# Two layers of a hybrid decoder step: decode chain reordered, page turns over three banks, heads paired

## The reference

```python
def trunk_layer(h, p, pos0, past, weights):
    a = rmsnorm(h, g_attn)
    qa, ka, va, qi, ki, wi, qb, kb, vb, u = split_columns(a @ w_in)
    qa, ka, qi, ki = ...            # QK-norm of qa, ka; rotary of all four
    # A: indexer scores, top-k keys, softmax over the chosen keys
    score = einsum('bqhs,bqh->bqs', relu(einsum('bqhd,bsd->bqhs', qi, ki) * 64 ** -0.5), wi)
    sel = top_k(where(causal, score, -inf), min(256, L // 4))
    o_a = softmax(qa . k_sel / 8) @ v_sel                   # 6 query heads, 2 KV heads
    # B: stick-breaking attention, 6 heads
    z = einsum('bqhd,bshd->bhqs', qb, kb_f) / 8
    log_rem = where(strict, log_sigmoid(-z), 0)
    o_b = exp(where(strict, z + reverse_cumsum(log_rem), -inf)) @ vb_f
    # C: causal pooling mixer
    o_c = pool_mix(u_ext, pos, w_pool, pool_scale)
    h = h + concat(o_a, o_b, o_c) @ w_out
    y, new_conv = conv_ffn(rmsnorm(h), conv_prefix, w_up, conv_w, conv_b, w_down)
    h = h + y
    return h + sigmoid(rmsnorm(h) @ w_ple_gate) * (p @ w_ple_proj), ...
```

## Time and profile before

| | us |
|---|---|
| median of 3 runs | 1666.86 (1665.31 to 1668.43) |
| the profiled execution | 1670.36 |
| its span | 1668.6 |
| TensorE busy | 1594.0 (96%) |
| VectorE, ScalarE, GpSimd busy | 885.2, 684.4, 274.9 |
| mean granted clock of TensorE | 0.969 |

### The profile page before, as it was taken

The page is one execution under the profiler, slowest core; times in us unless marked ns, Lnnn a source line. Parts: engine busy times, 40 slices in busy tenths (PEclk is TensorE's granted clock), DMA queues, the critical chain, the costliest instruction groups (busy, mean ns, idle before and its releaser), DMA issues.

```text
span 1668.6 us, 30587 instructions
## 1 busy us (share of the span) xinstructions
PE 1594.0 (96%) x11750; PEld 1439.5 (86%) x11750; DVE 885.2 (53%) x1558; ACT 684.4 (41%) x989; POOL 274.9 (16%) x472
## 2 busy tenths in 40 slices
PE   7999978899999999999999999879999999999998
PEld 5787845699999999999978786458999999999998
DVE  6657885135555553322847588632455555522335
ACT  4444546244444442224443344543444444422241
POOL 3320250011111110000105105201111111100000
PEclk8999979799999999999999999879999999999999
DMA  5233043132233323323223311341233323233221
GB/s 174 57 91 83 26 138 90 36 89 79 85 88 88 88 85 97 91 83 89 77 80 93 103 39 54 91 106 52 76 89 88 88 87 89 77 101 92 86 77 59
DMA packets 225719, 140.24 MB, mean 84 GB/s; under 512 B 13122, under 2 KB 219604, under 8 KB 225552
## 3 DMA queue, kind: packets, MB, share of 16 engines
q1 hardware_dynamic: 223220, 133.46, 27.9%
q0 software_dynamic: 2400, 5.42, 1.1%
HBM read 131.21 MB, written 7.65 MB: 83 GB/s over the span
## 4 chain that ended last, share of the span: by engine, by line
PE 80%; DVE 11%; issue 3%; ACT 3%; SPq 1%; DMA 1%; POOL 0%; DVEq 0%; ACTq 0%; POOLq 0%
PE ps L1679 23%; PE ps L1681 23%; PE ps L1680 23%; DVE score L1342 2%; DVE m L1339 2%; DVE w_L L1241 1%; PE ps L1742 1%; PE ps L1828 1%; DVE Lb L1413 1%; PE ps L2073 1%; PE ps L1928 1%; DVE stat L1460 1%; PE ps L1706 1%; PE ps L1838 1%; PE ps L1840 1%
## 5 line engine op out<-in xcount | busy, mean ns | idle before, releaser
L1679 PE MATMUL ps<-bH,w_H 128*128 128x272 f32 x1664 | 481.0, 289 | 4.6 <-DVE w_L L1241 3.2
L1241 DVE TENSOR_TENSOR w_L<-w_raw,w_H 128x1024 fp32r<-128x1024 f32 (+4 forms) x236 | 257.3, 1099 | 422.9 <-ACT w_H L871 422.2
L1681 PE MATMUL ps<-bH,w_L 128*128 128x272 f32 x1664 | 479.6, 288 | 0.0
L1680 PE MATMUL ps<-bL,w_H 128*128 128x272 f32 x1664 | 477.8, 287 | 0.0
L871 ACT ACTIVATE w_H<-w_raw 128x1024 fp32r<-128x1024 f32 (+4 forms) x236 | 220.1, 943 | 286.8 <-PE ps L1681 286.5
L1679 PEld LDWEIGHTS ps<-bH,w_H 128*128 128x128 f32 x1664 | 312.5, 188 | 6.3 <-DVE w_L L1241 4.1
L1680 PEld LDWEIGHTS ps<-bL,w_H 128*128 128x128 f32 x1664 | 313.6, 188 | 0.1
L1681 PEld LDWEIGHTS ps<-bH,w_L 128*128 128x128 f32 x1664 | 312.6, 188 | 0.0
L1679 PE MATMUL ps<-actH,w_H 128*128 128x272 f32 x704 | 204.2, 290 | 0.0
L1681 PE MATMUL ps<-actH,w_L 128*128 128x272 f32 x704 | 203.8, 289 | 0.0
L1680 PE MATMUL ps<-actL,w_H 128*128 128x272 f32 x704 | 202.7, 288 | 0.0
(11 more groups left out here) (329 smaller groups left out, 2344.0 us busy)
## 6 DMA issues: line engine op xcount, KB each, us to landing
w_raw<-in_w_up SPq DMA_DIRECT2D x88, 512.0 KB, 3.8
w_raw<-in_w_down SPq DMA_DIRECT2D x32, 512.0 KB, 3.9
w_raw<-in_w_in SPq DMA_DIRECT2D x24, 512.0 KB, 4.5
w_raw<-in_w_ple_gate SPq DMA_DIRECT2D x16, 512.0 KB, 3.9
w_raw<-in_w_down SPq DMA_DIRECT2D x16, 384.0 KB, 3.4
w_raw<-in_w_out SPq DMA_DIRECT2D x16, 320.0 KB, 3.4
w_raw<-in_w_in SPq DMA_DIRECT2D x8, 452.0 KB, 3.9
w_raw<-in_w_in SPq DMA_DIRECT2D x8, 384.0 KB, 3.2
```

The source lines that it names most:

```text
L1241: ins = dve.tensor_tensor(w_L[u % SPLIT][:, a:b], w_raw[raw_slot(l, u)][:, a:b], w_H[u % SPLIT][:, a:b].bitcast(F32), ALU.subtract)
L1679: pe.matmul(out, wh, xh, start=start, stop=False)
L1680: pe.matmul(out, wh, xl, start=False, stop=False)
L1681: return pe.matmul(out, wl, xh, start=False, stop=stop)
```

## The change

1. `index` computes two heads at a time, one on each half of the rows, into banks 7 and 0, and comes at six places, not twelve.
2. `logits` computes both heads of a pair, alternating, into banks 0 to 2 and 3 to 5. It waits for both exponentials and the copy of the pair before, and for the first pair for `f_ev` 3 and for the last relu.
3. VectorE's list: `weigh` in steps of two, six top-k rounds of tile 1 between them (two before); the later rounds move up, and three of them stand in the softmax, not five. `decode_queries` comes at u = 4, not 6.
4. Page turns go over three banks (5, 7, 4).
5. The state turns stand behind the value products, ahead of the turns of `o_s`. Behind the products of `bias_d` stand 14 filler products of 512 bf16 columns into bank 7, whose result nobody reads. The value products and the outputs lie in banks 4 to 6.
6. The first two output units begin with blocks 6 and 7, ahead of the wait for `d_lo`.

The diff, cut:

```diff
+        PAGE_BANK = [5, 7, 4]
+        I_BANK = [7, 0]
...
@@ ScalarE
-                        act.activation(relu_s[:, n % 2, 0:P * (t + 1)], ps[:, 7, 0:P * (t + 1)], ACT.Relu,
+                        act.activation(relu_s[:, n % 2, 0:P * (t + 1)], ps[:, I_BANK[e % 2], 0:P * (t + 1)], ACT.Relu,
...
-                    copy(KT[:, q % 8, :], ps[:, 5 - q % 2, :]).then_inc(kt_ev, 1)
+                    copy(KT[:, q % 8, :], ps[:, PAGE_BANK[q % 3], :]).then_inc(kt_ev, 1)
...
-                act.wait_ge(st_tr, at(st_tr, 1))
-                copy(stT[:, :, :], ps[:, 7, 0:KF * 2 * NB].rearrange("p (f b) -> p f b", b=2 * NB)).then_inc(st_ev, 1)
                 for g in range(2):
                     act.wait_ge(d_o, at(d_o, g + 1))
-                    copy(o_s[:, g, :], ps[:, 2 + g, :]).then_inc(d_oc, 1)
+                    copy(o_s[:, g, :], ps[:, 4 + g, :]).then_inc(d_oc, 1)
                 act.wait_ge(d_ot, at(d_ot, 1))
                 for out, of in decode_outputs(aH):
                     copy(out, of).then_inc(d_hi, 1)
+                act.wait_ge(st_tr, at(st_tr, 1))
+                copy(stT[:, :, :], ps[:, 7, 0:KF * 2 * NB].rearrange("p (f b) -> p f b", b=2 * NB)).then_inc(st_ev, 1)
@@ VectorE
-                weigh(1, 0, 3)
+                weigh(1, 0, 2)
                 feature_out(0)
-                weigh(1, 3, 4)
+                weigh(1, 2, 4)
                 split(14)
-                weigh(2, 0, 3)
+                select(1, 0, 2)
+                weigh(2, 0, 2)
+                select(1, 2, 3)
+                weigh(2, 2, 4)
                 feature_out(1)
-                weigh(2, 3, 4)
                 split(15)
-                select(1, 0, 1)
-                weigh(3, 0, 1)
-                select(1, 1, 2)
-                weigh(3, 1, 3)
+                select(1, 3, 5)
+                weigh(3, 0, 2)
+                select(1, 5, 6)
+                weigh(3, 2, 4)
                 feature_out(2)
-                weigh(3, 3, 4)
                 split(16)
...
-                    if u < 5:
-                        select(3, 11 + u, 12 + u)
-                    elif u == 6:
+                    if u < 3:
+                        select(3, 13 + u, 14 + u)
+                    elif u == 4:
                         decode_queries()
@@ TensorE
                 for t in range(1, 4):
                     for half in range(2):
                         feature(t - 1, half, 0, 4)
-                        index(t, 2 * half)
+                        if t > 1:
+                            index(t, 2 * half)
+                        elif half:
+                            index(1, 0)
                         feature(t - 1, half, 4, KD)
-                        index(t, 2 * half + 1)
+                    if t == 1:
+                        index(1, 2)
...
+                def logits(q):
+                    pe.wait_ge(f_ev, at(f_ev, 2 * q + 2 if q else 3))
+                    if q == 0:
                         pe.wait_ge(p_ev, at(p_ev, 15))
+                        pe.wait_ge(i_relu, at(i_relu, 12))
+                    else:
+                        pe.wait_ge(b_exp, at(b_exp, 2 * q))
+                        pe.wait_ge(b_cp, at(b_cp, q))
                     for i in range(4):
+                        for n in range(2):
+                            rows = slice(HD * n, HD * n + HD)
+                            pe.matmul(bz(n, i), featT[rows, F_KB + q, P * i:P * i + P], featT[rows, F_QB + q, P * i:TP],
+                                      start=i != 3, stop=False, skip_group_check=True)
...
+                    if q == 2:
+                        pe.wait_ge(o_lo, at(o_lo, 4))
...
+                    if q >= 3:
+                        pe.wait_ge(kt_ev, at(kt_ev, q - 2))
...
                     for b in range(4):
-                        mm = pe.transpose(ps[:, 5 - q % 2, P * b:P * b + P], k_page(q)[:, P * b:P * b + P], ident)
+                        mm = pe.transpose(ps[:, PAGE_BANK[q % 3], P * b:P * b + P], k_page(q)[:, P * b:P * b + P], ident)
...
-                pe.wait_ge(st_ld, at(st_ld, 16))
-                hold(pe)
-                for f in range(KF):
-                    mm = pe.transpose(ps[:, 7, 16 * f:16 * f + 16], st_tok[:, P * f:P * f + P], ident[0:16, 0:16])
-                mm.then_inc(st_tr, 1)
                 pe.wait_ge(d_bias, at(d_bias, 1))
                 for g in range(2):
                     mm = pe.matmul(ps[:, g, 0:KEYS_S], rep_bf[:, P * g:P * g + P], bias_d[:, :], **g_)
                 mm.then_inc(d_log, 1)
+                for _ in range(14):
+                    pe.matmul(ps[:, 7, :], id_bf, con_bf[:, :, :].rearrange("p a n -> p (a n)"), start=True, stop=True)
                 pe.wait_ge(d_sp, at(d_sp, 1))
...
-                pe.wait_ge(st_ev, at(st_ev, 1))
+                for m in range(2):
+                    pe.wait_ge(w_lo, at(w_lo, RAW + U_OUT + m + 1))
+                    dense(2 * m, U_OUT + m, (6, 7), aH, aL, True, False, c0=6 * P)
                 pe.wait_ge(d_lo, at(d_lo, 4))
...
-                    dense(2 * (m % 3), u, range(KD), aH, aL, True, True).then_inc(w_used, 1)
+                    dense(2 * (m % 3), u, range(6 if m < 2 else KD), aH, aL, m >= 2, True).then_inc(w_used, 1)
```

78 lines of the change are left out of this document (39 added, 39 removed).

## The result

| | before | changed |
|---|---|---|
| median of the runs, us | 1667.6 (1665.3 to 1668.4, 4 runs) | 1631.3 (1627.3 to 1633.5, 4 runs) |
| profiled execution, us | 1670.4, span 1668.6 | 1632.0, span 1630.2 |
| ratio, 95% interval | | 0.9773, 0.9756 to 0.979 |

What follows compares the result with a forecast made beforehand. TensorE, 80% of the last-ending chain, was taken as the bound. Pairs 7.2, page turns 2.2 and decode chain 11.1 or 13.7 us gave 20.5 and 23.1 a layer, 43.6 off the 1666.9 median: 1623.3 us, range 1611 to 1640.

Steps and rivals of the forecast that it cites:

- Pairs and their three givebacks: Indexer pairs save 4.9 us, logits pairs 7.05, less 1.3 and 3.0 given back: 7.7 us at the remainders of pair 2.
- First wait: Ahead of the first logits, TensorE stands 1.3 us more for feature_out(2), between 0.7 and 2.5.
- The waits ahead of the remainders: In the three logits pairs, ScalarE's chain and VectorE's queue give back 0.4, 1.0 and 1.6 us, 3.0 in all.
- The 0.5 us that I left for VectorE behind pair 2: Behind pair 2 VectorE is late again with six rounds of 512, costing 0.5 us: 7.2 us a layer remain.
- Softmax: Two top-k rounds leaving and decode_queries two steps earlier, taken at nothing; up to 3.5 us if TensorE's cover fails.
- Page turns: Page turns over three banks save 2.2 us a layer, bounds 1.0 and 3.2.
- Decode chain: Turns of z to 48 dense matmuls: 22.5 us; after 2.1 taken off for the clock, saves 11.1 and 13.7.
- 13.7 us in layer 1: Saving from the turns of z to the first output unit in layer 1, from 38.3 us; bounds 2.5 and 15.8.
- Rival 1: Narrow products let the clock fall right behind the fillers; decode chain brings 0 and 2.5 us: 1645; chance 0.15.
- The slower rival: Waits ahead of each pair's remainders pull the clock down in the stick-breaking stage: 1689 us; chance 0.03.
- The rival that prices PSUM Bottleneck: Pairs bring nothing, since the way over ScalarE and VectorE takes everything back: 1638 us; chance 0.12.
- The better rival: The clock never falls (4.2 us) and the softmax gains (up to 7): 1614 us; chance 0.10.

Runs made afterwards that it cites:

- feature_before_weigh: The changed kernel with feature_out(2) ahead of the last weigh step instead of behind it; 1631.0 us, ratio 0.9771 to the kernel before.
- page_turns_two_banks: The changed kernel with the page turns over two banks again (5 and 4); 1636.3 us, ratio 0.98 to the kernel before.
- queries_in_the_gap: The changed kernel with decode_queries moved earlier, just ahead of row_max(5), beside VectorE's longest wait; 1625.9 us, ratio 0.9746 to the kernel before.
- after_again: The changed kernel itself, unaltered, run once more beside later kernels; 1629.3 us, ratio 0.976 to the kernel before.
- pairs_alone: The kernel before with only the indexer and logits pairs and VectorE's new order; 1654.4 us, ratio 0.9908 to the kernel before.
- three_edits: The changed kernel with decode_queries in VectorE's gap, feature_out(2) ahead of the last weigh step, state turns behind the pool blocks; 1622.0 us, ratio 0.9713.
- heads_unpaired: The changed kernel with indexer products one by one and logits head after head, VectorE's new order kept; 1659.9 us, ratio 0.9947 to the kernel before.
- decode_alone: The kernel before with all of the change except the pairs and VectorE's new order; 1647.4 us, ratio 0.9872 to the kernel before.

## Why the prediction held, and where it missed

**Pairs and their three givebacks: the sum right, its parts less so.** Forecast 7.7 us at the remainders of pair 2, measured 7.73 and 7.69. Of what the pairs save, the indexer's part came out as forecast: without the wait ahead of them, the first logits come 4.8 us earlier in both layers (4.9 forecast). First wait 1.3 forecast, 1.76 and 1.40 measured. The waits ahead of the remainders were to be 0.4, 1.0 and 1.6; layer 0 has 0.36, 0.61 and 1.39, so their cost was put 0.6 too high and the first wait 0.1 to 0.5 too low. That the sum is right to 0.1 us is in part luck: the two misses cancel. The Trainium skill (TensorEngine Tiling, Theoretical Speedup) allows up to twice the speed for at most 64 rows, and the trace agrees: 2.43 us for sixteen records, 2.42 for eight. The same page says under PSUM Bottleneck that tiling doesn't speed up the emptying of PSUM, which may become the limit after a fourfold speed-up. Here, at twofold, the waits took back 4.1 of the 12 us in layer 0 (1.76 at the first logits, 2.36 ahead of the remainders), not all. They are waits for VectorE instructions that read PSUM, but stand in its queue behind weigh steps and top-k rounds: moving one weigh step took the first from 1.76 to 0.91 us (feature_before_weigh). The 0.5 us that I left for VectorE behind pair 2 did not come.

**Softmax: sign missed, small.** Taken at nothing, it lost 0.6 us a layer. I had costed the two top-k rounds that leave, but neither the bias that moves forward with the end of the rounds (0.6 us at unit 3) nor the 2.15 us of decode_queries, which took the place that the rounds gave up. With decode_queries out of the way it took 1.1 and 2.9 us less than in the profile of before; part of the 2.9 is a short low stretch that only the latter has.

**Page turns: right.** First products 3.96 us behind the first turn (4.0 forecast), last group 10.86 (11.0), 2.3 us in all (2.2). Layer 1 gained the same 2.3 up to the products of the new keys, and then lost 2.6 to the stall and the clock behind it.

**Decode chain: every term near but the clock.** To the triangle 3.89 (3.85 forecast), triangle 2.84 (2.6), P_d 0.86 (0.95), value products 6.26 (6.2), state turns 1.46 (1.25), turns of o_s 3.14 (1.6) and the 48 dense matmuls 7.81 (6.05), the last two largely at 0.50 clock, for which 2.1 us had been set aside. Where the clock stays up the chain takes 23.1 us (page_turns_two_banks, queries_in_the_gap), where my sum said 22.5. Over the seven profiles of the changed order of this chain layer 0 took 23.1 to 27.9, in the middle 24.7: the sum with the 2.1 us taken off for the clock, 24.6, is that middle. Layer 1 took 26.2 to 27.5, in the middle 27.2. Of those 2.5 us more, about 1 is the stall, behind which the triangle mostly starts late (4.95 us in after_again); the rest is the low stretch behind the value products, which lasts 6.8 us in six of the seven layers 1 but in only two of the seven layers 0. One of the six is feature_before_weigh, where the stall did not pull the clock down, so why layer 1 has the longer one is open.

**The step that was off** is "13.7 us in layer 1": it assumed that layer 1 runs as layer 0 does, and that it starts from a dearer old order (38.3 us). The new order has a stall there that no row of before showed, and a longer low stretch. The old order is not dearer in layer 1 either (34.8 us in pairs_alone), but that did not make the miss, since forecast and table use the same profile of before. Page turns and chain of layer 1 brought 10.1 us where I had 15.9, which is 5.8 of the 7.9 us that were missing once the 2.7 of the start are taken out; the rest is 1.9 in layer 0 (its profile had a longer low stretch than the middle one) and 1.2 in the softmax, less 1.0 for what was left at pair 2. In each layer 0.4 of it is my own: I took the unit as 48 matmuls in the sum and used windows that end three later.

**Rivals.** Rival 1 came only in part. In ten profiles layer 0 has the fillers at the full clock ahead of the triangle. In eight of them the clock stayed at 1.00 until the value products were done; in two (feature_before_weigh at 282.7, three_edits at 281.7) it fell just behind the triangle, for 3.4 us. The run without fillers shows what it would have been like. The slower rival did not come either, but heads_unpaired shows its mechanism.

Three slips of the working changed little. The rival that prices PSUM Bottleneck is the second, not the third. The better rival's own terms give 1612, not 1614. And VectorE's counts (27.5 against 26.7, 28.2 against 26.5) give 0.8 and 1.7 us, where the sum has 1.0 and 1.6; measured is 27.3 and 27.9 us from remainders to remainders. The kernel before had no wait of TensorE at pair 2, though VectorE came to that clamp straight from a top-k round.

## What to carry to other kernels

Cost a reordered stretch at the full clock and add what the clock does as a term with its own spread (here the same instructions took 23.1 to 27.9 us); fillers in a wait that can't be removed were worth 9 us, and cost nothing where they ended before it did (in layer 1, at half clock, they ended late). Before a loss is put down to what was moved, look at where the lost time begins: here it began ahead of the piece that was blamed. When work is moved on a second engine, price all that arrives in its new place as well as what leaves. Do a part alone as well as undoing it: the two can differ, here by a factor of two, when undoing a part leaves others that were fitted to it and lets the clock fall.

## What the runs showed of the hardware

**A stall at a count of instructions.** TensorE stood 0.66 to 1.6 us in layer 1 in all 13 profiles of a kernel with any part of the change, among the products of the new keys. Eight of them have it ahead of the same matmul record. Adding 3 or taking away 14 records in layer 0 moved it by just as many. But it also came 4 records later in decode_alone and 6 later in heads_unpaired, which have as many matmuls as the changed kernel and differ in order and in waits: so matmul records alone are not the count. In all 13 profiles queue q8, of the kind that the profile calls instruction, carried one packet 2.2 to 2.9 us before TensorE went on, and the one before it came at least 8.4 us before. In the changed kernel the DMA queues of 1069.25 to 1070.25 us show (packets, MB, share of 16 engines)

```profile
q8 instruction: 1, 0.02, 5.9%
```

The reading that fits is that TensorE ran out of instructions just where its smallest products (32 columns, 51 records in 0.6 us) use them up fastest; no run tried it by itself. The Trainium skill (Runtime: NRT & Kernel Launch, Terms) says that each engine's instruction memory is refilled in blocks of 16 KiB, which agrees with the packet's 0.02 MB. Why before shows no such stall is open. One may lie under a wait: before has such a packet at 1099.7 us, and 2.6 us later, at 1102.26, TensorE begins the turns of z, for which it waited 0.50 us on ScalarE.

**The clock has its own luck.** With the same instructions in the stretch, the start (103.7 to 106.4 us), the softmax of the new order (50.7 to 54) and the chain behind the turns of z (23.1 to 27.9) vary by some us each, with where the low stretches of granted clock lie and how long they last. That is about the spread of the runs, 1627 to 1634 us for the changed kernel, and it is why the single edits were read from their stretches and not from their totals.
